# Down projection by seven half products instead of eight, with four weight sums made in DRAM

## The chip, the cores and the metric

One core of a Trainium2 chip runs the whole kernel as one program. It has five engines, each with its own instruction stream: TensorE (PE in the rows; PEld is its loading of weights), VectorE (DVE), ScalarE (ACT), GpSimd (POOL) and SyncE (SP), which issues transfers. Instructions of an engine run in the order written; engines wait for each other by semaphores. Data lies in SBUF (128 partitions), in PSUM (eight banks of 128x512 fp32 that TensorE writes), and in DRAM. The metric is device microseconds of one execution.

## The reference

One layer of a decoder on 1024 tokens of width 1024: a mixer, then a gated MLP. The change touches the last product of the MLP and the addition behind it:

```python
def conv_gated_mlp(x, w_up, conv_w, w_down):
    h = causal_dwconv(x @ w_up, conv_w)
    gt, val = jnp.split(h, 2, axis=-1)
    return (jax.nn.silu(gt) * val) @ w_down
...
x = x + rms_norm(conv_gated_mlp(h, ffn_w_up[l], ffn_conv_w[l], ffn_w_down[l]), norm_ffn_post[l])
```

The inner width is 2816, so the last product is (1024 x 2816) times (2816 x 1024), in fp32. rms_norm divides each row of 1024 by its root mean square and multiplies by a gain.

## The kernel before, in words

An fp32 product is done as two passes of a reduced format: a weight tile w is split into a high part (ScalarE copies it with a scale, `dn_split_hi`, L2306) and a low part (w minus the high part, `dn_split_lo`, L2316, on VectorE or POOL); the activations likewise (`act_split_hi`, L2351, on ScalarE; `act_split_lo`, L2355, on VectorE). A pair of matmuls, high by high and low by low with the scales chosen so that both add to the product, goes into a PSUM bank (`pair`, L2490).

The down projection takes the tokens in two halves of four tiles (m = 0, 1) and the inner width in 22 blocks of 128 (k). A step kk = (m, k) loads 128x1024 weights from DRAM, splits them, splits 128x512 activations, and does 4 tiles x 2 column halves x 2 parts = 16 matmuls. Two PSUM banks belong to a tile, so a half uses all eight. Weights and activations go through rings of four buffers: the high part of step kk waits until TensorE is through with step kk - 4. The activations of the up projection were spilled to DRAM (`act_mid`) and come back by `act_reload`. In the up projection before it, which is already done by seven products a slab, POOL makes the low parts (`split_mult_lo`, L2102), VectorE the sums of weights from SBUF (`weight_sum`, L2225) and the sums in PSUM (`added`, L2232). The order of the up stage, with the first three steps of the down projection in it, is a list written out by hand (`UP_ORDER`: e loads weights, f and g split them, i and j split activations, t, c, v, y, p are the convolution and gate).

After a half, `norm` (ScalarE) squares and sums a row and takes the inverse root, `finish` (VectorE) multiplies by it and by the gain, `add` adds the input of the MLP (x1r, reloaded from DRAM), and SP stores. The last tile is done in two column halves (L2411 on ScalarE, L2442 and L2450 on VectorE), the last but one by POOL (`down_pool`, L2481).

In the mixer, POOL's part for token tile t (0 to 7) begins with `A1b` (`scaled`, L1005, twice), then `A3a` (L1028, L1030, and L1032 behind ScalarE's L1168) and `B1` (L1022, used by VectorE's L1346). SP issues the small transfers of the mixer (L915, L927).

## Time and profile before

| | us |
|---|---|
| three runs: lowest, median, highest | 1059.56, 1063.14, 1063.42 |
| the profiled execution | 1061.33 |
| its span | 1059.6 |
| TensorE busy | 1023.5 (97%) |
| VectorE busy | 814.0 (77%) |
| ScalarE busy | 634.9 (60%) |
| POOL busy | 500.8 (47%) |

A busy time is the time in which an engine had an instruction running; TensorE's instructions overlap, so two matmuls may stand 0.23 us apart and be listed with 0.39 each. A line's idle time before it is put down to what released it last.

### The profile page before, as it was taken

Reading aid. Unit: us, or ns where it says so; the run is one execution under the profiler, and the core shown is the slowest. Engines: PE = TensorE matmul, PEld = TensorE weight load, DVE = VectorE, ACT = ScalarE, POOL = GpSimd, SP = SyncE. Lnnn points to the kernel's source line nnn. Section 1 sums busy time; section 2 is a strip of 40 time slices with the busy share of each in tenths; the row PEclk is TensorE's granted clock in tenths of the full one; section 3 lists DMA queues with packets and bytes.
Section 4 is the critical chain, followed back from the end, with each engine's and each line's share of the span. In section 5 each row is a group of like instructions: output and inputs, shape, how many; then the busy total and the mean of one; then the engine's idle time right before and its main releaser. Section 6 shows DMA issues by size and latency. Waiting matters only on the chain.

```text
span 1059.6 us, 19099 instructions
## 1 busy us (share of the span) xinstructions
PE 1023.5 (97%) x7136; PEld 831.5 (78%) x7136; DVE 814.0 (77%) x1140; ACT 634.9 (60%) x1201; POOL 500.8 (47%) x653
## 2 busy tenths in 40 slices
PE   5999999998999999999999999999999998999997
PEld 4878878986777778777688787888887786888885
DVE  5798895756668886877586598899999999646755
ACT  7544423347777777777865455666666667446443
POOL 2457423726454565551410278788788886000000
PEclk9999999999999999999999999999999999999999
DMA  8245311352122112012263612234433335955962
GB/s 274 71 128 171 115 52 27 75 121 58 41 60 60 36 44 60 19 29 61 90 222 126 199 41 80 80 123 129 130 126 122 121 110 210 371 170 182 331 240 80
DMA packets 159523, 126.78 MB, mean 120 GB/s; under 512 B 63908, under 2 KB 137928, under 8 KB 159432
## 3 DMA queue, kind: packets, MB, share of 16 engines
q1 hardware_dynamic: 157992, 120.32, 37.8%
q10 hardware_dynamic: 1440, 5.24, 1.2%
q8 instruction: 58, 0.95, 0.4%
q14 instruction: 33, 0.27, 0.1%
HBM read 99.79 MB, written 25.71 MB: 118 GB/s over the span
## 4 chain that ended last, share of the span: by engine, by line
PE 57%; DVE 9%; issue 4%; POOL 4%; ACT 3%; DMA 0%; DVEq 0%; ACTq 0%; POOLq 0%
PE psum L2490 14%; PE psum L2278 9%; PE psum L1786 5%; PE psum L1735 5%; PE psum L1719 4%; POOL slab_q L2102 4%; PE psum L1551 4%; PE psum L1901 3%; PE psum L1702 3%; PE psum L2284 2%; DVE arena L2186 2%; DVE arena L2180 1%; DVE arena L2225 1%; DVE psum L2232 1%; PE psum L1632 1%
## 5 line engine op out<-in xcount | busy, mean ns | idle before, releaser
L2102 POOL TENSOR_TENSOR slab_q<-arena,slab_p 128x512 fp32r<-128x512 f32 x127 | 208.2, 1668 | 45.5 <-ACT slab_p L2095 45.4
L2490 PE MATMUL psum<-dn_p,ap_p 128*128 128x512 f32 x352 | 110.3, 393 | 2.7 <-DVE arena L2186 1.4
L2490 PE MATMUL psum<-dn_q,ap_q 128*128 128x512 f32 x352 | 109.8, 391 | 0.0
L2278 PE MATMUL psum<-t_p,slab_p 128*128 128x512 f32 x272 | 106.3, 391 | 1.3 <-ACT arena L2159 0.8
L2278 PE MATMUL psum<-t_q,slab_q 128*128 128x512 f32 x272 | 105.9, 389 | 0.0
L2095 ACT ACTIVATE slab_p<-arena 128x512 fp32r<-128x512 f32 x127 | 78.2, 628 | 38.7 <-PE psum L2278 13.8
L2316 DVE TENSOR_TENSOR dn_q<-arena,dn_p 128x1024 fp32r<-128x1024 f32 x41 | 50.2, 1224 | 56.3 <-ACT dn_p L2306 56.3
L1431 DVE CUSTOM_DVE_ANT_0 psum<-psum,arena 128x640 f32<-128x640 f32 (+7 forms) x96 | 67.8, 717 | 29.8 <-PE psum L1702 29.2
L2306 ACT ACTIVATE dn_p<-arena 128x1024 fp32r<-128x1024 f32 x44 | 46.6, 1059 | 70.0 <-PE psum L2490 65.6
L3066 PE MATMUL psum<-h_p,cm_p 128*128 128x512 f32 (+1 forms) x288 | 86.4, 372 | 0.6 <-DVE arena L2973 0.6
L3066 PE MATMUL psum<-h_q,cm_q 128*128 128x512 f32 (+1 forms) x288 | 85.8, 371 | 0.0
L2278 PE MATMUL psum<-h_p,slab_p 128*128 128x512 f32 x204 | 79.8, 391 | 0.7 <-POOL slab_q L2102 0.6
L2490 PEld LDWEIGHTS psum<-dn_p,ap_p 128*128 128x128 f32 x352 | 65.7, 188 | 18.8 <-issue 2.5
L1219 ACT ACTIVATE arena<-psum,arena 128x640 f32<-128x640 f32 (+7 forms) x96 | 67.1, 701 | 21.5 <-DVE arena L1431 20.7
L2278 PE MATMUL psum<-h_q,slab_q 128*128 128x512 f32 x204 | 79.4, 389 | 0.0
L2481 POOL TENSOR_TENSOR arena<-arena 128x1024 f32<-128x1024 f32 x1 | 2.4, 2356 | 160.6 <-DVE arena L2454 160.6
L2490 PEld LDWEIGHTS psum<-dn_q,ap_q 128*128 128x128 f32 x352 | 66.1, 188 | 14.6
L2951 DVE SCALAR_TENSOR_TENSOR arena<-psum,arena 128x1023 f32<-128x1023 f32 (+29 forms) x60 | 75.9, 1265 | 1.4
L1226 ACT ACTIVATE arena<-psum 128x384 f32<-128x384 f32 x132 | 60.1, 488 | 22.6 <-PE psum L1719 21.3
L2225 DVE TENSOR_TENSOR arena<-arena 128x512 f32<-128x512 f32 x68 | 72.6, 1083 | 0.0
L2591 POOL TENSOR_TENSOR cm_q<-arena,cm_p 128x1024 fp32r<-128x1024 f32 x16 | 39.1, 2443 | 60.8 <-ACT cm_p L2586 60.7
L1735 PE MATMUL psum<-arena 128*64 128x192 f32 x528 | 63.4, 345 | 1.7 <-ACT arena L1226 1.7
(321 smaller groups left out, 2632.3 us busy)
## 6 DMA issues: line engine op xcount, KB each, us to landing
arena<-in_ffn_w_up SPq DMA_DIRECT2D x44, 512.0 KB, 5.2
arena<-in_ffn_w_down SPq DMA_DIRECT2D x44, 512.0 KB, 4.0
arena<-in_w_in SPq DMA_DIRECT2D x20, 512.0 KB, 3.9
act_mid<-arena SPq DMA_DIRECT2D x18, 512.0 KB, 2.6
arena<-act_mid SPq DMA_DIRECT2D x36, 256.0 KB, 5.0
arena<-in_x SPq DMA_DIRECT2D x16, 512.0 KB, 4.8
qkv_mid<-arena ACTq DMA_DIRECT2D x9, 512.0 KB
arena<-qkv_mid SPq DMA_DIRECT2D x8, 576.0 KB, 4.6
```

The source lines that it names most:

```text
L1219: act.activation(probs(u), s_psum(u, n), ACT.Exp, scale=-1.0, bias=nmx[:, u % 2:u % 2 + 1], accum_out=psums[:, NH * kind + h:NH * kind + h ...
L1226: act.activation(pt[x % 2].rearrange("p g c -> p (g c)"), psum[:, bank, 0:GDIM], ACT.Copy).then_inc(done, 1)
L1431: v.tensor_tensor_reduce(out=s_psum(u, n), in0=s_psum(u, n), in1=hidden, scale=-1.0, scalar=-NEG, op0=ALU.add, op1=ALU.min, accum_out=nmx[ ...
L1735: ins = pe.matmul(psum[tok, 7, 0:GDIM // 2], val[:, b, kind, HD * kv:HD * (kv + 1)], pt[x % 2][:, :, tok], start=b == k0, stop=True, skip_ ...
L1786: ins = pe.matmul(wm_ps[WM_SLOT[t]][:, n * 512:(n + 1) * 512], x[:, k], w[:, n * 512:(n + 1) * 512], start=first and k == ks[0] and w is w ...
L2095: act.activation(slab_p[n % RING], part_source(i, j), ACT.Copy, scale=1.0 - SPLIT_W).then_inc(late("up_hi")[0], 1)
L2102: pool.tensor_tensor(slab_q[n % RING], part_source(i, j), slab_p[n % RING], ALU.subtract).then_inc(late("up_lo")[0], 1)
L2225: v.tensor_tensor(out, x, y, op).then_inc(late("s_add")[0], 1)
L2278: ins = pe.matmul(mult_ps(i, j), w[:, k], x[:, k], start=k == 0 and x is x_p[i] and i in (1, 2, 5), stop=True, skip_group_check=True)
L2490: ins = pe.matmul(dn_ps[t % HT][:, n * 512:(n + 1) * 512], x[:, tok], w[:, n * 512:(n + 1) * 512], start=first and x is ap_p[s], stop=True ...
L2951: own.up(v.scalar_tensor_tensor(out=cacc[:, c, s:S], in0=glu[c][:, 0:S - s], scalar=w, in1=cacc[:, c, s:S], op0=ALU.mult, op1=ALU.add))
L3066: ins = pe.matmul(cm_ps[i % 2][:, c0:c1], w[:, k], x[:, k, c0:c1], start=k == 0 and x is h_p, stop=True, skip_group_check=True)
```

## The change

The down projection is written as a 2x2 block product: tokens in two halves, the inner width in two halves of 11 blocks (HK = 11), the columns of the result in two halves of 512. By Strassen's scheme in Winograd's form seven products of half matrices replace eight. They are taken in the order 1, 2, 6, 5, 7, 3, 4, each of 11 steps, so a step n runs from 0 to 76. A step loads 128x512 weights, splits them and 128x512 activations, and does 4 tiles x 2 parts = 8 matmuls of the same shape as before. Weight buffers are a ring of eight half tiles, activation buffers still one of four.

The products need sums of blocks on both sides. The four sums of weights are made in DRAM (`w_sums`, four arrays of 1408x512 fp32, 2.88 MB each) by eight transfers that POOL issues in the mixer, right after `A1b` of tiles 0, 2, 4, 5, 6 and 7: copies, and transfers that add to what lies there. The sums of activations are made in place in SBUF in steps 16 to 27: on VectorE `third` (L2536) and `second` (L2545), on POOL `minus` (L2605) and `fourth` (L2610). The weights' low parts are POOL's in steps 0 to 15 and in every even step from 40, VectorE's else (L2366 on either; L2435 is now `act_split_lo`).

Two sets of four PSUM banks take the products in turn. Between products ScalarE copies a set to SBUF (`copied_out`) or VectorE adds what was copied to it and writes a quarter of the result (`joined`, L2551, L2554, L2558). Squares and row sums come quarter by quarter (L2496 on ScalarE), and POOL multiplies by the gain (`weighted`, L2614). At the end POOL adds two sums of squares (L2631) and two tiles of the input (L2637); VectorE finishes two tiles of the first half (L2582) and all of the second (L2591 from PSUM, L2598). The first six steps stand in the hand-written order of the up stage, where three stood.

```diff
+HK = NF // 2
+DN_MULTS = (1, 2, 6, 5, 7, 3, 4)
+DN_STEPS = [(i, k) for i in DN_MULTS for k in range(HK)]
+DN = len(DN_STEPS)
+W_RING, A_RING = 8, 4
+UP_TAIL = 6
+DN_POOL_LO = [n for n in range(DN) if n < 16 or (n >= 40 and n % 2 == 0)]
+DN_DVE_LO = [n for n in range(DN) if n not in DN_POOL_LO]
...
-    "h3.21 i0 l3.21 e1 a2.21 f0 v0.20 i1 g0 k7.21 v1.20 y20 a5.21 i2 p20 f1 t1.21 g1 j0 j1 x20 f2 a3.21 c1.21 t0.21 g2 v1.21 c0.21 "
-    "v0.21 y21 p21 "
+    "h3.21 i0 l3.21 a2.21 f0 f1 b0 v0.20 i1 g0 g1 k7.21 v1.20 y20 a5.21 e2 e3 i2 p20 b1 t1.21 j0 j1 x20 e4 e5 f2 j2 g2 i3 f3 g3 a3.21 "
+    "j3 c1.21 t0.21 i4 f4 g4 j4 v1.21 i5 f5 g5 j5 c0.21 v0.21 y21 p21 "
...
+        def down_sums(pool, t):
+
+            w11, w12, w21, w22 = [a["ffn_w_down"][0, h * HK * P:(h + 1) * HK * P, c * HALF_D:(c + 1) * HALF_D] for h in range(2) for c in range(2)]
+            one, two, three, four = [w_sums[n] for n in range(4)]
+            if t == 0:
+                pool.dma_start(one, w11).then_inc(sem("wt"), 16)
+                pool.dma_start(three, w12).then_inc(sem("wt"), 16)
+            elif t == 2:
+                pool.wait_ge(sem("wt"), 32)
+                pool.dma_start(one, w12, accum_op=ALU.add).then_inc(sem("wt"), 16)
+                pool.dma_start(three, w22, accum_op=ALU.add).then_inc(sem("wt"), 16)
+            elif t == 4:
+                pool.wait_ge(sem("wt"), 64)
+                pool.dma_start(two, one).then_inc(sem("wt"), 16)
+            elif t == 5:
+                pool.wait_ge(sem("wt"), 80)
+                pool.dma_start(two, w22, accum_op=ALU.add).then_inc(sem("wt"), 16)
...
                 scaled(kg[t % 2], kn, EG, t).then_inc(sem("g_kk2"), 1)
+                down_sums(pool, t)
...
+            if n >= A_RING:
+                act.wait_ge(*late("dn_mm", n - A_RING + 1))
...
+            def third(k):
+                act_landed(v, 0, k)
+                act_landed(v, 1, k)
+                v.tensor_tensor(quarter(0, k), quarter(0, k), quarter(1, k), ALU.subtract).then_inc(late("d_s")[0], 1)
...
+            for n in range(UP_TAIL, DN):
+                for i, at_ in ((2, 26), (7, 59), (3, 70)):
+                    if at_ <= n < at_ + 2:
+                        joined(i, 2 * (n - at_))
+                        joined(i, 2 * (n - at_) + 1)
+                if n in DN_DVE_LO:
+                    dn_split_lo(v, n)
+                act_split_lo(v, n)
+                if 16 <= n < 16 + HK:
+                    third(n - 16)
+                if 17 <= n < 17 + HK:
+                    second(n - 17)
...
+            def minus(k):
+                row_sum_done(pool, "S3", k)
+                act_landed(pool, 1, k + HK)
+                pool.tensor_tensor(quarter(1, k), quarter(1, k + HK), quarter(1, k), ALU.subtract).then_inc(late("d_z")[0], 1)
+
+            def fourth(k):
+                row_sum_done(pool, "S2", k)
+                pool.wait_ge(*late("ap_lo", DN_STEPS.index((2, k)) + 1))
+                pool.tensor_tensor(quarter(0, k + HK), s2[k % len(s2)], quarter(0, k + HK), ALU.subtract).then_inc(late("d_z")[0], 1)
...
+            for n in range(UP_TAIL, 40):
+                if n in DN_POOL_LO:
+                    dn_split_lo(pool, n)
+                if 17 <= n < 17 + HK:
+                    minus(n - 17)
+                    fourth(n - 17)
...
+            pool.wait_ge(*late("f_sq", 3 * HT))
+            pool.tensor_tensor(wrs[:, 2 * HT:3 * HT], wss[:, 0:HT], wss[:, HT:2 * HT], ALU.add).then_inc(late("f_b")[0], 1)
+            for t in range(HT):
+                weighted(c12[t], 2 * HT + t + 1, right_d)
...
+            own_k = 4
+            for n in range(DN - own_k):
+                i, k = DN_STEPS[n]
+                ready(n)
+                for t in range(HT):
+                    if k == 0:
+                        free(i, t)
+                    ins = pair(n, t, k == 0 and i in (1, 2, 5))
+                ins.then_inc(late("dn_mm")[0], 1)
+            for t in range(HT):
+                for n in range(DN - own_k, DN):
+                    if t == 0:
+                        ready(n)
+                    ins = pair(n, t, False)
+                ins.then_inc(late("dn_t")[0], 1)
```

What stands on VectorE in the middle of the down projection before, for some two steps (dn_p and dn_q are the high and low part of the weights, ap_p and ap_q of the activations; arena is any other SBUF; the number behind a name tells the buffers apart):

```order
L2316 TENSOR_TENSOR dn_q_146<-arena,dn_p_142 128x1024
L2355 SCALAR_TENSOR_TENSOR ap_q_154<-ap_p_150,arena 128x512
L2462 TENSOR_TENSOR arena<-arena 128x1024
L2316 TENSOR_TENSOR dn_q_147<-arena,dn_p_143 128x1024
L2355 SCALAR_TENSOR_TENSOR ap_q_155<-ap_p_151,arena 128x512
```

And on VectorE in steps 17 and on now:

```order
L2366 TENSOR_TENSOR dn_q_154<-arena,dn_p_146 128x512
L2435 SCALAR_TENSOR_TENSOR ap_q_162<-ap_p_158,arena 128x512
L2536 TENSOR_TENSOR arena<-arena 128x512
L2545 TENSOR_TENSOR arena<-arena 128x512
L2366 TENSOR_TENSOR dn_q_155<-arena,dn_p_147 128x512
L2435 SCALAR_TENSOR_TENSOR ap_q_163<-ap_p_159,arena 128x512
```

Where a step had one instruction for its weights and one for its activations, and only now and then an addition, a step of half the matmuls now has four.

POOL from the end of the up projection to its last instruction before, where the additions to the last but one tile (L2481) are all that it does after three low parts of weights:

```order
L2102 TENSOR_TENSOR slab_q_171<-arena,slab_p_166 128x512
L2316 TENSOR_TENSOR dn_q_145<-arena,dn_p_141 128x1024
L2316 TENSOR_TENSOR dn_q_146<-arena,dn_p_142 128x1024
L2316 TENSOR_TENSOR dn_q_147<-arena,dn_p_143 128x1024
L2481 TENSOR_TENSOR arena<-arena 128x1024
```

POOL now, around step 15:

```order
L2366 TENSOR_TENSOR dn_q_154<-arena,dn_p_146 128x512
L2366 TENSOR_TENSOR dn_q_155<-arena,dn_p_147 128x512
L2366 TENSOR_TENSOR dn_q_156<-arena,dn_p_148 128x512
L2605 TENSOR_TENSOR arena<-arena 128x512
L2610 TENSOR_TENSOR arena<-arena 128x512
```

And at the end of its program, from step 73 on:

```order
L2614 TENSOR_TENSOR arena<-arena 128x512
L2366 TENSOR_TENSOR dn_q_151<-arena,dn_p_143 128x512
L2366 TENSOR_TENSOR dn_q_153<-arena,dn_p_145 128x512
L2631 TENSOR_TENSOR arena<-arena 128x4
L2614 TENSOR_TENSOR arena<-arena 128x512 x4
L2637 TENSOR_TENSOR arena<-arena 128x1024 x2
```

POOL has instructions through the whole stage now: low parts of weights, eleven pairs of L2605 and L2610 in a row, products with the gain, and at the very end seven instructions in a chain.

POOL at token tile 0 of the mixer before (L1028 and L1030 are `A3a`):

```order
L1002 TENSOR_TENSOR arena<-arena 128x32
L1011 TENSOR_TENSOR arena<-arena 128x48
L1005 TENSOR_TENSOR arena<-arena 128x384 x2
L1028 TENSOR_TENSOR arena<-arena 128x384
L1030 TENSOR_TENSOR arena<-arena 128x384
```

And now, where the same lines are L1050, L1074 and L1076:

```order
L1047 TENSOR_TENSOR arena<-arena 128x32
L1056 TENSOR_TENSOR arena<-arena 128x48
L1050 TENSOR_TENSOR arena<-arena 128x384 x2
L1019 DMA w_sums<-in_ffn_w_down 1408x512
L1020 DMA w_sums<-in_ffn_w_down 1408x512
L1074 TENSOR_TENSOR arena<-arena 128x384
L1076 TENSOR_TENSOR arena<-arena 128x384
```

Two issues of 1408 rows of 512 stand in front of what used to follow at once.

## Rows read from the trace of the kernel before

**Rows 1.** Page, part 1: span; busy time, share and instructions of each engine.

```profile
span 1059.6 us, 19099 instructions
PE 1023.5 (97%) x7136; PEld 831.5 (78%) x7136; DVE 814.0 (77%) x1140; ACT 634.9 (60%) x1201; POOL 500.8 (47%) x653
```

**Rows 2.** Chain of waits, in order: start us, us, what; the down projection.

```profile
898.65 139.32 PE psum L2490 x608
1041.12 12.24 PE psum L2490 x52
```

**Rows 3.** Windows, down: PE, PEld, DVE, ACT, POOL busy (count); clock, DMA, GB/s.

```profile
888.00:898.00 10.00, 8.31 (x33) 5.59 (x31) 8.80 (x8) 4.01 (x5) 4.20 (x2) 1.00 0.82 278
898.00:1038.00 140.00, 139.35 (x609) 114.47 (x610) 82.55 (x89) 69.08 (x96) 0.00 (x0) 1.00 0.70 253
1038.00:1053.40 15.40, 14.95 (x64) 11.56 (x62) 8.79 (x9) 7.14 (x17) 0.58 (x1) 1.00 0.17 69
1053.40:1059.60 6.20, 0.00 (x0) 0.00 (x0) 2.29 (x3) 1.16 (x4) 1.78 (x1) 0.70 0.44 169
```

**Rows 4.** Page, part 5: the down projection's matmuls, one of two forms.

```profile
L2490 PE MATMUL psum<-dn_p,ap_p 128*128 128x512 f32 x352 | 110.3, 393 | 2.7 <-DVE arena L2186 1.4
```

**Rows 5.** Timeline, the end of the down stage; idle time and releaser in brackets.

```profile
1041.09 0.30 PEld L2490 LDWEIGHTS psum<-dn_p,ap_p 128*128 128x128 f32 x2 [0.78 <-DVE dn_q L2316]
1052.82 2.36 POOL L2481 TENSOR_TENSOR arena<-arena 128x1024 f32<-128x1024 f32 x1 [160.62 <-DVE arena L2454]
1052.95 0.39 PE L2490 MATMUL psum<-dn_q,ap_q 128*128 128x512 f32 x1
1054.70 1.68 DVE L2450 SCALAR_TENSOR_TENSOR arena<-arena 128x512 f32<-128x512 f32 x2
```

**Rows 6.** Single lines: ns least/median/greatest, first and last start, form.

```profile
L2225 DVE TENSOR_TENSOR arena<-arena x68: 674/937/1820, 658.6 to 879.8; 128x512 f32<-128x512 f32 x68
L2232 DVE TENSOR_TENSOR psum<-psum,arena x51: 681/686/700, 675.7 to 889.9; 128x512 f32<-128x512 f32 x51
L2102 POOL TENSOR_TENSOR slab_q<-arena,slab_p x127: 1282/1527/3380, 617.7 to 881.6; 128x512 fp32r<-128x512 f32 x127
L2355 DVE SCALAR_TENSOR_TENSOR ap_q<-ap_p,arena x44: 682/684/2896, 886.4 to 1040.3; 128x512 fp32r<-128x512 f32 x44
L2095 ACT ACTIVATE slab_p<-arena x127: 613/631/637, 613.3 to 880.6; 128x512 fp32r<-128x512 f32 x127
```

**Rows 7.** Timeline of POOL and VectorE (DVE), 872 to 883 us: start, us, instruction.

```profile
872.89 10.00 POOL L2102 TENSOR_TENSOR slab_q<-arena,slab_p 128x512 fp32r<-128x512 f32 x6 [2.47 <-ACT slab_p L2095]
873.47 2.97 DVE L2225 TENSOR_TENSOR arena<-arena 128x512 f32<-128x512 f32 x2
```

**Rows 8.** Timeline, mixer, around the places of POOL's new transfers.

```profile
234.66 1.00 POOL L1030 TENSOR_TENSOR arena<-arena 128x384 f32<-128x384 f32 x1
236.43 0.51 ACT L1168 ACTIVATE arena<-arena 128x384 f32<-128x384 f32 x1
289.21 0.83 POOL L1022 TENSOR_TENSOR arena<-arena 128x384 f32<-128x384 f32 x1 [3.72 <-PE psum L1612]
293.48 0.74 DVE L1346 TENSOR_TENSOR arena<-arena,psum 64x192 f32<-64x192 f32 x2 [0.60 <-PE psum L1623]
387.78 1.61 POOL L1005 TENSOR_TENSOR arena<-arena 128x384 f32<-128x384 f32 x2 [1.70 <-DVE arena L1300]
422.29 1.62 POOL L1005 TENSOR_TENSOR arena<-arena 128x384 f32<-128x384 f32 x2 [3.97 <-DVE arena L1300]
```

**Rows 9.** Issue of transfers on SP: ns least/median/greatest.

```profile
L915 SPq DMA_DIRECT2D arena<-tri_mid x8: 308/331/1556, 241.9 to 466.0; - x8
L927 SPq DMA_DIRECT2D arena<-inv_mid x16: 580/612/627, 258.5 to 482.8; - x16
```

**Rows 10.** Windows, early mixer (columns as in Rows 3).

```profile
250.00:255.00 5.00, 3.71 (x23) 2.14 (x21) 3.49 (x12) 4.34 (x15) 4.09 (x14) 0.88 0.00 0
254.00:255.00 1.00, 1.00 (x8) 0.68 (x4) 0.00 (x0) 0.95 (x5) 0.73 (x4) 0.50 0.00 0
```

More of the change, by code:

```diff
@@ new lines, in down_loads @@
+            for t in (0, 1):
+                sp.wait_ge(sem("fin_v"), t + 1)
+                sp.dma_start(out[0, t * P:(t + 1) * P, :], y_dn[:, t]).then_inc(sem("stored"), 16)
+            for t in (2, 3):
+                sp.wait_ge(*late("fin_p", t - 1))
+                sp.dma_start(out[0, t * P:(t + 1) * P, :], y_dn[:, t]).then_inc(sem("stored"), 16)
+            for t in range(HT, NT - 1):
+                sp.wait_ge(sem("fin_v"), t - 1)
+                sp.dma_start(out[0, t * P:(t + 1) * P, :], y_dn[:, t]).then_inc(sem("stored"), 16)
@@ new lines, in copied_out, with squares @@
+            def copied_out(i, t):
+                product_done(act, i)
+                if i == 1 and t == 0:
+                    act.wait_ge(*late("up_mm", 2 * CLASSIC + PRODUCTS))
+                act.activation({1: c11, 6: c12, 5: c22}[i][t], acc_of(i)[t], ACT.Copy).then_inc(late("e_cp")[0], 1)
+            def squares(n, x, before):
+                if before:
+                    act.wait_ge(*late("f_sq", before))
+                act.activation(junk2[:, left_d], x, ACT.Square, accum_out=wss[:, n:n + 1]).then_inc(late("f_sq")[0], 1)
```

464 lines of the change are left out of this document (250 added, 214 removed), and 2 rows, old and new, of the table UP_ORDER.

## The prediction

> **What bounds the kernel now.** I read the page first, then the chain of waits, then the windows of the down projection, then single lines by duration, and last the timelines of VectorE and POOL side by side. The page has TensorE busy for 97% of the span, so only two things move the time: fewer or cheaper matmuls, and gaps between them [rows 1]. The chain shows the down projection as one run of TensorE: 608 matmuls in 139.32 us, 0.229 us each, and after one short stop 52 more [rows 2]. All its 704 matmuls (two forms of 352) stand between 888.0 and 1053.4 us [rows 3, 4]. 704 x 0.229 is 161.3 us, so 4.1 of these 165.4 us are gaps, 1.7 of them in the first 10 us (8.31 of 10 busy). POOL has nothing to do from 898 to 1052 us, VectorE is 59% busy, ScalarE 49% [rows 3]. The last VectorE instruction ends at 1056.4, 3.0 us after the last matmul, and the store of that half ends the span at 1059.6 [rows 5].
>
> **What is removed.** Seven products of eleven steps n, each of four token tiles and two matmuls: 616 matmuls against 704, of the same 128x512 form. 88 x 0.229 = -20.2 us. A step is 8 x 0.229 = 1.83 us of TensorE. Product 1 needs only the four banks of the second last slab, where the old order soon came to the banks of the last one; I keep 1 us of the 4.1 us of gaps for the new head (bounds 0 and 4.1): -3.1 us.
>
> **What is added on VectorE and POOL, and what it collides with.** This is the term that decides. First what they charge alone: a two-input VectorE instruction of 128x512 takes 0.67 to 0.68 us (least of L2225, median of L2355), and starts about 0.60 after the one in front, as they overlap a little; a POOL one 1.28 us (least of L2102), 1.25 from start to start [rows 6]. But L2225 reaches 1.82 us and L2102 has a median of 1.53. The timelines say why: POOL needs 10.0 us for six instructions that alone take 7.7, and inside that stretch two L2225 in a row take 2.97 us instead of 1.35 [rows 7]. Each of the two waited for a POOL instruction to end, and POOL waited in turn. L2232, which reads one operand from PSUM and one from SBUF, stays between 0.681 and 0.700 in all 51 cases although POOL is as busy [rows 6]. So I add the times of instructions with two SBUF inputs on VectorE and of POOL's, one after the other, wherever both have work; before, POOL had none in this stretch.
>
> Steps 17 to 27. VectorE has four such instructions a step (weight low part, activation low part, L2536, L2545), POOL two (L2605, L2610), and POOL's two wait for VectorE's two of the same step, so neither can be put off far. That is 4 x 0.60 + 2 x 1.25 = 4.9 us a step where TensorE wants 1.83. Eleven steps: 53.9 us against 20.2. The ring of four activation buffers lets VectorE be three steps ahead, 5.5 us. +28.2 us. Bounds: without any lead +33.7; if VectorE never waited for POOL, 11 x 2.4 = 26.4, and 2.4 for the four additions from PSUM that fall in steps 26 and 27, less 20.2 and 5.5: +3. I take the upper half, since the rows show the pair taking turns.
>
> The Trainium skill speaks against the change here: "SBUF — State Buffer", section "Who interferes with whom", says that a VectorE instruction with two SBUF inputs and a POOL instruction that reads SBUF hold a shared port by turns, each for its whole length, and that with one SBUF input VectorE does not meet POOL at all. The 2.97 us and the steady 0.69 us agree. By a reading in which both only slow each other a little, this term would be the +3 above.
>
> Steps 59 to 74. Activation low part 0.60, every other step a weight low part on VectorE (0.60) or POOL (1.25), every other step one L2614 on POOL (1.25): 2.15 us a step on average, 0.32 over TensorE's 1.83, sixteen times, less what lead is left: +4 us (0 to 5). Steps 28 to 58 need 1.2 to 1.6 us and hide behind TensorE; so do ScalarE's two splits a step (0.63 each at most) and its 12 copies and 12 squares.
>
> Last four steps. TensorE takes them tile by tile and wants all four activation buffers at once, which are freed only by step 72; the old kernel stops there for 0.8 us on the weight side [rows 5]. With the port shared, I take 2.5 us more (0 to 3.8).
>
> **The end.** POOL's L2631 needs the squares of the last quarter, which ScalarE issues in steps 73 to 76, some 8 us before TensorE ends. Behind it stand on POOL four L2614 (1.25 each) and two additions of 128x1024 (2.36 by L2481 [rows 5]), 9.7 us; on VectorE two L2582 and three L2598 of 128x1024 (1.2 each, double the 0.60) and two halves, 7.2 us. All read two SBUF operands. 17 us of turns from -7.4 end at +9.6, with the multiplications from PSUM between them at about +11.5, against +3.0 before: +8.5 us (bounds: +4, where only ScalarE's and VectorE's own chains count, and +12).
>
> **The sums of weights.** Eight transfers of 2.88 MB are issued by POOL during the mixer. Does POOL wait for them? A copy reads and writes 5.8 MB, an accumulation reads twice and writes, 8.7 MB; at the 253 GB/s of the down stage [rows 3] that is 23 and 34 us. The tightest step, from tile 5 to tile 6, is 34.5 us (387.78 to 422.29 [rows 8]), for one accumulation. So no wait or a very short one. What the issue costs POOL is not in the trace, since no transfer of before is issued there. The nearest rows are SP's: 0.33 us for one of 48 x 16 runs, 0.61 for one of 64 x 6 [rows 9]; the far bound is the time in which POOL would walk over the same elements, 1408x512 over 128 partitions at 2.36 us per 1024, 13 us. I take 2 us for each of the six with 1408 rows, nearer SP's, and 1 us for the two flat copies. Behind them stand on POOL: at tile 0 L1028 and L1030, whose result ScalarE's L1168 uses 0.8 us after they end, so 2 x 2 us come out as 3; at tile 2 L1022, which has 3.7 us of idle ahead of it and 3.4 us behind it until VectorE's L1346 wants it, so nothing comes out [rows 8]; at the other four about 1 us together. +4 us (0 to 62).
>
> The Trainium skill's "DMA: Bandwidth & Descriptors", section "Anatomy of one DMA — SWDGE (gpsimd) path", calls the generation of descriptors small and variable and gives 2.0 us and bytes over 436e3 for a transfer; by that alone this term would be near 0. No row here shows it.
>
> **TensorE's clock.** In the mixer the granted clock fell to 0.50, the 1.2 GHz level, for some 3.5 us around 255 us, in a stretch in which TensorE was busy for 3.71 of 5 us [rows 10]. In steps 17 to 27 it will be busy for 1.83 of 4.9. At half speed a step is 3.7 us, still under 4.9, so nothing is lost there; the first microseconds behind it may run at half: +1 us (0 to 5).
>
> **Sum.** -20.2 - 3.1 + 28.2 + 4 + 2.5 + 8.5 + 4 + 1 = +24.9 us on the profiled execution of 1061.33 us (its span of 1059.6 and 1.7 around it; the median of the runs shown is 1.8 above it): 1086 us.
>
> **Rivals.**
> The two engines do not hold each other up, because VectorE's instructions go first or POOL's fall into its gaps. Then the terms are -20.2 - 3.1 + 3 + 0 + 0 + 4 + 4 + 0 = -12.3: 1049 us. For it: the rows show waits where POOL had come first, not who wins when both stand ready, and L2610's result is wanted only from step 55. Against it: L2610 and L2605 stand on POOL in front of the weight parts of step 40 and are ready to run at once, so they do run there. 17%. Half blocked, it would lie within 5 us of before: 8%.
>
> Issuing from POOL is dear. At 13 us for each of the six, tile 0 shows 25, tile 2 19 (26 less 7), tiles 5 and 7 about 11 each: 66 us instead of 4, 1148 us; it decides from some 3.5 us each, where the 7 us of room at tile 2 are used up; at 6 us each it is 25 us and 1107. For it: POOL has no row that says otherwise. Against it: SP's rows do not grow with the number of runs. 15%.
>
> The forecast itself: 60%. That the sums come too late is no case: the last is issued at tile 7 of the mixer, and the first load that needs one comes in step 22 of the down projection, hundreds of microseconds later.
>
> **Chances and range.** Below 0.5% (5 us) a measurement of this kernel can hardly tell a change from none. Faster 18% (the first rival), within 0.5% 8%, slower 74%. The forecast's own range is 1068 to 1105 (its terms at their inner bounds). The range runs down to the first rival and into the second: 1050 to 1118.
>
> **What would show it.** In the profile after: 616 matmuls still 0.229 us apart where TensorE runs freely; L2536 and L2545 on VectorE well above 0.68 us on average, L2605 and L2610 above 1.28; TensorE near 40% busy for about 48 us in the second fifth of the down stage, waiting for VectorE's activation or weight low parts; the down stage some 177 us from first to last matmul; some 14 us from the last matmul to the end. L2366 and L2435 at 0.68 us throughout and no gap in TensorE would prove the first rival; idle ScalarE or TensorE at 234 and 286 us, behind POOL's transfers, the second. I am wrong if POOL's instructions run without holding VectorE up, or if the mixer grows by more than 10 us.

## The result, and the profile after

The changed kernel takes 1146.70 us (median of 4 runs, 1146.43 to 1147.66) against 1062.81 for the kernel before in the same comparison: a ratio of 1.080 with a 95% interval of 1.078 to 1.082. Slower was forecast, but 1086 us, and 1146.7 is outside the range of 1050 to 1118.

The page of the changed kernel, part 1, answers to [rows 1]: span, then busy time, share and instructions of each engine.

```profile
span 1145.9 us, 19413 instructions
PE 1032.9 (90%) x7048; PEld 832.1 (73%) x7048; DVE 881.6 (77%) x1202; ACT 661.7 (58%) x1289; POOL 612.0 (53%) x729
```

88 matmuls are gone, and yet TensorE idles for 113 us instead of 36. Where, four marks tell: the first matmul of the output projection, the first and the last of the down projection, and the end of the span.

| us from the span's start | before | after | difference |
|---|---|---|---|
| output projection starts | 524.9 | 589.7 | +64.8 |
| down projection starts | 888.0 | 953.1 | +65.1 |
| down projection, first to last matmul | 165.4 | 178.0 | +12.6 |
| from there to the end | 6.2 | 14.8 | +8.6 |

So 65 of the 86 us come from the mixer, where the change only adds eight transfers. The mixer as one window of each kernel (columns as in [rows 3]); first before, then after:

```profile
225.00:524.90 299.90, 291.59 (x3732) 226.70 (x3726) 217.15 (x552) 221.93 (x577) 149.23 (x334) 0.99 0.22 50
```

```profile
225.00:589.70 364.70, 308.99 (x3740) 240.40 (x3734) 221.84 (x552) 222.66 (x577) 157.20 (x342) 0.90 0.47 105
```

VectorE, ScalarE and POOL do the same work as before to within 8 us; TensorE's busy time grows by 17 us at a lower granted clock (0.90 instead of 0.99). What doubled is the DMA side. The waits of the changed kernel from 225 to 640 us (who waited for whom: us in total, times, the longest), and below them the first one as it was before:

```profile
POOL arena L1090 <- DMA arena<-tri_mid: 62.1, 5, 17.4
ACT arena L1265 <- DVE arena L1477: 53.7, 28, 20.3
...
PE psum L1597 <- DMA arena<-invt_mid: 33.2, 3, 19.0
```

```profile
POOL arena L1044 <- DMA arena<-tri_mid: 27.8, 5, 7.6
```

The mixer sends small triangles to DRAM and back within its chain (`tri_blocks` and `inverse_back`, on SP's queue). While a bulk transfer runs, they come back late. The timeline of the changed kernel around POOL's second pair of bulk transfers; POOL issues two accumulations, then SP stores the inverse and loads it again only 21 us later:

```profile
298.88 1.53 POOL L1023 DMA_DIRECT2D w_sums<-in_ffn_w_down  x1
299.80 2.14 POOL L1024 DMA_DIRECT2D w_sums<-in_ffn_w_down  x1
...
305.94 0.30 SPq L942 DMA_DIRECT2D inv_mid<-arena  x1
306.28 0.54 SPq L942 DMA_DIRECT2D invt_mid<-arena  x1
327.35 1.25 SPq L948 DMA_DIRECT2D arena<-inv_mid  x2
```

How long the eight pairs of stores of the inverse took to land, after and before:

```profile
DMA to landing us min/median/max: 1.9/2.2/21.0
...
DMA to landing us min/median/max: 1.9/2.1/2.2
```

The store of tri_mid landed in 2.3 / 5.4 / 15.2 us against 2.3 / 2.3 / 3.7. The DMA queues of the changed kernel show why; q0 is POOL's, q1 SP's (packets, MB, and the time of the packets as a share of the 16 engines' time, above 100% where packets overlap), from 306 to 310 us, from 315 to 320 and from 320 to 325:

```profile
q0 software_dynamic: 366, 0.75, 109.7%
q1 hardware_dynamic: 17, 0.00, 0.7%
...
q0 software_dynamic: 504, 1.00, 108.3%
q1 hardware_dynamic: 504, 0.03, 15.8%
...
q0 software_dynamic: 496, 1.02, 109.1%
q1 hardware_dynamic: 496, 0.03, 15.5%
```

In the last two stretches the two queues move packet for packet. A small store of 48 KB in runs of 16 numbers is 768 packets of 64 bytes; each waits for one packet of 2 KB. 1536 of them, for the two stores, at 100 a microsecond are 15 us. In the kernel before, the same queue moved 1155 packets of such a pair in the one microsecond from 257 to 258. The Trainium skill says this in "DMA: Bandwidth & Descriptors", section "Queues, rings and completion order": each DMA engine goes round its queues packet by packet. The trace agrees, with 504 to 504.

Turns do not explain all of it. From 306 to 310 us SP's queue moved only 17 packets, although both stores had been issued by 306.8: some 4 of the 21 us pass before the packets begin. And beside the first two copies SP's queue moved 216 packets to POOL's 439 from 240 to 246 us, and only then, from 246 to 252, as many as POOL's (473 to 475).

The rest of the profile came out near the forecast. The down projection of the changed kernel in windows (columns as in [rows 3], whose stage they answer to):

```profile
953.00:985.00 32.00, 28.39 (x118) 22.85 (x117) 28.24 (x23) 21.93 (x38) 22.18 (x14) 0.95 0.92 326
985.00:1035.00 50.00, 32.81 (x108) 23.24 (x107) 50.00 (x50) 16.12 (x28) 35.08 (x22) 0.83 0.43 138
1035.00:1060.00 25.00, 24.17 (x106) 19.55 (x105) 18.93 (x29) 16.60 (x30) 3.52 (x3) 1.00 0.52 157
1060.00:1090.00 30.00, 30.00 (x133) 24.57 (x132) 19.09 (x25) 22.75 (x45) 12.15 (x10) 1.00 0.49 168
1090.00:1131.00 41.00, 38.86 (x161) 29.01 (x159) 39.08 (x37) 25.65 (x52) 32.65 (x21) 1.00 0.44 160
1131.00:1145.90 14.90, 0.08 (x1) 0.00 (x0) 9.50 (x9) 5.55 (x17) 5.28 (x3) 0.64 0.62 247
```

From 985 to 1035 us VectorE is busy for all 50 us and TensorE has matmuls in flight for 32.8. Its instructions there, of the changed kernel (ns least/median/greatest, first and last start), answer to [rows 6]: L2435 is the activations' low part, L2536 `third`, L2605 `minus`, L2610 `fourth`, L2551 the addition that reads PSUM.

```profile
L2435 DVE SCALAR_TENSOR_TENSOR ap_q<-ap_p,arena x77: 674/693/1852, 951.5 to 1123.1; 128x512 fp32r<-128x512 f32 x77
L2536 DVE TENSOR_TENSOR arena<-arena x11: 679/1761/1781, 984.4 to 1028.7; 128x512 f32<-128x512 f32 x11
L2605 POOL TENSOR_TENSOR arena<-arena x11: 1673/1724/1740, 985.2 to 1031.3; 128x512 f32<-128x512 f32 x11
L2610 POOL TENSOR_TENSOR arena<-arena x11: 1279/1652/1674, 988.7 to 1034.3; 128x512 f32<-128x512 f32 x11
L2551 DVE TENSOR_TENSOR arena<-psum,arena x4: 675/676/679, 1025.1 to 1030.5; 128x512 f32<-128x512 f32 x4
```

`third` takes 1.76 us instead of 0.68 beside `minus`, while L2551, which reads PSUM, keeps 0.68 in the same stretch.

The end answers to [rows 5]. POOL's timeline of the changed kernel (`weighted`, L2614, and the last additions, L2637), then ScalarE's (scaling of finished tiles, L2521, and squares, L2496), then VectorE's first finishing of a tile of the second half (L2598):

```profile
1124.69 6.98 POOL L2614 TENSOR_TENSOR arena<-arena 128x512 f32<-128x512 f32 x4
1131.64 4.63 POOL L2637 TENSOR_TENSOR arena<-arena 128x1024 f32<-128x1024 f32 x2
```

```profile
1131.71 1.15 ACT L2521 ACTIVATE arena<-arena 128x1024 f32<-128x1024 f32 x1 [1.00 <-POOL arena L2614]
1132.76 0.58 ACT L2496 ACTIVATE arena<-psum 128x512 f32<-128x512 f32 x1
```

```profile
1134.34 3.02 DVE L2598 SCALAR_TENSOR_TENSOR arena<-arena 128x1024 f32<-128x1024 f32 x1
```

ScalarE's first square of the last four tiles waits behind a scaling, and that for POOL, until 1.7 us after the last matmul has ended (1131.1). L2598, beside POOL's L2637, takes 3.02 us; the next two of its kind, with POOL at rest, take 1.28 each.

### The profile page after: what moved, and what is told of

The parts are those of the page before. It is cut to its first block and busy times, and to the rows that moved or that the text cites. A ratio compares the mean times of both kernels' runs of the same rounds, so it can differ in the third digit from the quotient of the medians.

```text
span 1145.9 us, 19413 instructions
## 1 busy us (share of the span) xinstructions
PE 1032.9 (90%) x7048; PEld 832.1 (73%) x7048; DVE 881.6 (77%) x1202; ACT 661.7 (58%) x1289; POOL 612.0 (53%) x729
## 5 line engine op out<-in xcount | busy, mean ns | idle before, releaser
L2648 PE MATMUL psum<-dn_p,ap_p 128*128 128x512 f32 x308 | 127.1, 413 | 23.8 <-DVE ap_q L2435 22.1
L2648 PE MATMUL psum<-dn_q,ap_q 128*128 128x512 f32 x308 | 125.1, 406 | 0.0
L2435 DVE SCALAR_TENSOR_TENSOR ap_q<-ap_p,arena 128x512 fp32r<-128x512 f32 x77 | 86.0, 1131 | 17.9 <-ACT ap_p L2431 17.7
L2648 PEld LDWEIGHTS psum<-dn_p,ap_p 128*128 128x128 f32 x308 | 60.4, 196 | 45.8 <-issue 25.8
L2431 ACT ACTIVATE ap_p<-arena 128x512 fp32r<-128x512 f32 x77 | 48.6, 631 | 61.9 <-PE psum L2648 51.3
L2366 POOL TENSOR_TENSOR dn_q<-arena,dn_p 128x512 fp32r<-128x512 f32 x35 | 52.0, 1497 | 57.5 <-ACT dn_p L2362 57.5
L1597 PE MATMUL psum<-arena 64*64 64x64 f32 x1152 | 48.4, 239 | 33.4 <-DMA arena<-invt_mid 33.2
L1597 PEld LDWEIGHTS psum<-arena 64*64 64x64 f32 x1152 | 42.4, 151 | 42.5 <-issue 40.6
L1765 PE MATMUL psum<-arena 128*128 128x128 f32 x396 | 64.7, 292 | 7.9 <-DVE arena L1490 7.2
```

What stands on the lines that cost most here:

```text
L1597: ins = pe.matmul(out[rows, h * CH:(h + 1) * CH], lhs[rows, h], rhs[rows, h], start=start, stop=True, skip_group_check=True)
L1765: ins = pe.transpose(psum[:, bank, g * P:(g + 1) * P], probs(u + g)[:, (b - k0) * P:(b - k0 + 1) * P], ident)
L2435: v.scalar_tensor_tensor(out=ap_q[n % A_RING], in0=ap_p[n % A_RING], scalar=1.0 - 1.0 / SPLIT_W, in1=act_part(n), op0=ALU.mult, op1=ALU.su ...
L2648: ins = pe.matmul(acc_of(i)[t], x[:, tok], w, start=first and x is ap_p[n % A_RING], stop=True, skip_group_check=True)
```

## The experiments

Theory A: the bytes of the bulk transfers on the shared DMA engines hold up the mixer's small transfers. Against it B (POOL's issuing or its waits) and C (accumulation as such). Theory D: VectorE and POOL take turns in steps 17 to 27. Against it E (VectorE's own load). All runs in one table: the marks of the profiled run, and the median time of 2 to 10 runs (before: 1063 to 1064 in each comparison). e1, e2 and e16 put plain blocks of weights in place of the sums, e3 and e4 leave parts of the sums out, so their output is not the reference's; the matmuls are the same in number and form.

| run | output proj. starts | down proj. starts | its length | to the end | time |
|---|---|---|---|---|---|
| after | 589.7 | 953.1 | 178.0 | 14.8 | 1146.7 |
| e1_no_sums | 525.6 | 889.0 | 180.3 | 14.9 | 1087.0 |
| e2_thin | 531.5 | 895.0 | 180.5 | 14.9 | 1091.8 |
| e3_plain | 569.5 | 933.1 | 179.1 | 14.9 | 1127.1 |
| e4_no_pool_sums | 586.9 | 950.5 | 156.9 | 14.9 | 1127.2 |
| e5_short_rows | 619.2 | 983.0 | 179.8 | 14.9 | 1180.1 |
| e6_moved | 526.0 | 939.1 | 178.9 | 14.9 | 1135.8 |
| e7_dve | 590.2 | 954.5 | 160.9 | 14.9 | 1132.1 |
| e8_both | 527.4 | 939.6 | 164.9 | 14.9 | 1120.1 |
| e9_pairs | 525.2 | 918.1 | 179.8 | 14.9 | 1114.2 |
| e10_tail | 589.2 | 952.7 | 185.6 | 8.6 | 1147.3 |
| e11_all | 524.2 | 915.0 | 168.3 | 10.2 | 1093.6 |
| e12_early | 560.4 | 923.8 | 180.7 | 14.8 | 1118.8 |
| e13_early_all | 560.7 | 924.8 | 163.8 | 11.4 | 1100.4 |
| e14_early_spread | 560.5 | 923.6 | 162.9 | 11.4 | 1098.9 |
| e15_cover | 533.1 | 916.8 | 165.1 | 11.4 | 1091.6 |
| e16_free_sums | 527.2 | 890.7 | 163.5 | 11.4 | 1067.2 |

**e1_no_sums.**

```diff
-                down_sums(pool, t)
...
-                return w_sums[WSUM_OF[i], k * P:(k + 1) * P, :]
+                return a["ffn_w_down"][0, k * P:(k + 1) * P, right_d if i in (5, 6) else left_d]
```

> Leaves out the eight transfers that make the sums of weights, and SyncE's wait for them; the four products that used the sums load plain blocks of the down weights instead, so the output is not the reference's. Everything else of the changed kernel stays. If the 65 us that the mixer became longer come from the sums of weights in any way, the output projection starts near 525 us again instead of 590 and the time is about 1146.7 - 65 = 1082 us (1078 to 1088). If something else of the change lengthened the mixer (another buffer, another place in memory), it stays near 1147 us.

1087.0 us, and the output projection starts at 525.6 again. The 65 us are the sums' (64.1 by this mark; 59.7 in the median time, and 2.3 of the difference because the down stage is longer in this run's profile). The rest of the change costs 23 us, where the forecast had 21 (24.9 without its 4 for the sums).

**e2_thin.**

```diff
-            one, two, three, four = [w_sums[n] for n in range(4)]
+            one, two, three, four = [w_sums[n][:, 0:16] for n in range(4)]
+            w11, w12, w21, w22 = [w[:, 0:16] for w in (w11, w12, w21, w22)]
...
```

> The same eight transfers of 1408 rows with the same waits and semaphores, but 16 columns of each row instead of 512: a 32nd of the bytes, the same number of rows to describe and of issues by GpSimd; the products load plain blocks of weights (the sums are left out of the computation). Theory A, that the bytes of the bulk transfers on the shared DMA engines hold up the mixer's small transfers: about 1085 us (1080 to 1095), stores of tri_mid land in 2.3 to 4 us again. Rival B, that GpSimd's issuing, the making of the descriptors or GpSimd's waits for the sums hold it up: 1140 to 1147 us. In between would mean that the number of rows counts as well as their bytes.

1091.8 us: with the same issues, waits and rows the mixer pays 6.6 us instead of 64.8. The transfers land sooner here, too, but in the changed kernel none of POOL's listed waits from 225 to 640 us is for one of them. So B falls. The DMA part of its page (KB each, median us to landing):

```profile
tri_mid<-arena SPq DMA_DIRECT2D x16, 96.0 KB, 2.3
...
w_sums<-in_ffn_w_down POOLq DMA_DIRECT2D x6, 88.0 KB, 4.2
```

**e3_plain.**

```diff
-                pool.dma_start(one, w12, accum_op=ALU.add).then_inc(sem("wt"), 16)
+                pool.dma_start(one, w12).then_inc(sem("wt"), 16)
...
```

> All eight transfers with all their bytes and waits, but as plain copies, none accumulating (sums left incomplete). In the trace an accumulating transfer lands after about 21 us and a plain one after 10.8 us when each runs alone. Theory A (bulk time on the DMA engines): the bulk's time falls from some 150 us to some 100 us, and the 65 us to about 40 to 45, so 1120 to 1127 us. Rival C, that only accumulation holds the small transfers up: 1082 to 1090 us. Rival B (issue and waits of GpSimd): 1146 us, or a little less because the waits end earlier.

1127.1 us; the mixer pays 44.6 us. The cost grows with the time for which the bulk occupies the engines: the eight landing times add up to 121.5 us here and to 152.2 in the changed kernel. C falls as the whole cause. Its DMA rows:

```profile
w_sums<-in_ffn_w_down POOLq DMA_DIRECT2D x6, 2816.0 KB, 14.5
...
tri_mid<-arena SPq DMA_DIRECT2D x16, 96.0 KB, 4.0
```

**e4_no_pool_sums.**

```diff
...
-                if 17 <= n < 17 + HK:
-                    minus(n - 17)
-                    fourth(n - 17)
```

> Leaves out the two sums of activations that GpSimd makes in each of steps 17 to 27 of the down projection (minus and fourth); the products 5 and 3 use unsummed rows. VectorE's own four instructions in a step stay. Theory D (VectorE and GpSimd take turns at their operands): VectorE's instructions there fall from 1.1 us to 0.68 us, a step from 4.9 us to 4 x 0.68 = 2.7 us, so 11 x 2.2 = 24 us less: the down projection takes 154 us from first to last matmul instead of 178, the time is about 1123 us (1119 to 1127). Rival E (VectorE is slow there by its own load alone): its instructions stay at 1.1 us and more, and the time at 1142 to 1147 us.

The stage takes 156.9 us instead of 178.0. Without POOL beside them, `third` and `second` (L2536, L2543 of this run) take 0.68 us each:

```profile
L2536 DVE TENSOR_TENSOR arena<-arena x11: 679/682/685, 982.6 to 1007.3; 128x512 f32<-128x512 f32 x11
L2543 DVE TENSOR_TENSOR arena<-arena x11: 679/682/683, 985.0 to 1010.9; 128x512 f32<-128x512 f32 x11
```

D holds with 21 us of the 24 expected, and E falls as the main cause. The edit also takes away VectorE's waits for `fourth`; in the changed kernel VectorE was busy for all 50 us from 985 to 1035, so it lost nothing to such waits.

**e5_short_rows.**

```diff
+            def short(out, x, **how):
+                for c in range(0, HALF_D, P):
+                    pool.dma_start(out[:, c:c + P], x[:, c:c + P], **how).then_inc(sem("wt"), 16)
...
```

> The changed kernel with the same sums and the same bytes, but each transfer cut into four of 128 columns, so that a packet of the bulk is 512 bytes instead of 2 KB or more; 32 issues instead of 8, at the same eight places. In the trace of the changed kernel the two queues move packet for packet while a bulk transfer runs (496 and 496 packets in 320 to 325 us), so a small transfer waits one bulk packet for each of its own. Theory A1 (packets in turn): with a bulk packet of about a quarter of the time, the stores of tri_mid and inv_mid that fall beside the bulk land in 4 to 9 us instead of 15 to 21, and the stalls shrink from 65 us to about 20. The 24 more issues at 0.6 to 2.1 us cost GpSimd up to 30 us, of which the mixer may show 5 to 20: together 1110 to 1130 us. Theory A2 (the small transfers share bandwidth, or stand behind the whole bulk): the stores land in 15 to 21 us as before and the time is 1150 us or more.

Neither forecast holds: the time, 1180.1 us, misses, and the landing times do not decide. The greatest of the inverse's store falls from 21.0 to 7.6 us, of tri_mid's from 15.2 to 11.4, which looks like packets taken in turn. But the store that took 7.6 us, issued at 345.5, moved its first packets behind 349 us, when the bulk was at its end (from 350 to 351 SP's queue moved 1068 packets, POOL's 137). And beside tri_mid's stores the edit hardly shortened the bulk's packets: from 248 to 252 us 331 packets carried 1.25 MB, 3.8 KB each, against 4.1 in the changed kernel (316 and 1.29 MB). So the turns stay untested by this run. What made it slower is new: POOL stands still between its issues, for nothing that the profile names. From this run's waits (225 to 640 us):

```profile
POOL w_sums L1021 <- issue: 43.5, 5, 12.3
```

32 issues of 1408 short rows in groups of four and eight were too many in flight, as it seems; that was not tried further.

**e6_moved** puts 32 pieces of 352 rows beside the up projection; **e7_dve** gives the 22 sums to VectorE; **e8_both** does both.

```diff
...
+            if n >= 8 and (n - 8) % 3 == 0 and (n - 8) // 3 < 32:
+                down_sums(pool, (n - 8) // 3)
```

```diff
...
+                if n == 26:
+                    fourth(0)
+                if 28 <= n < 28 + HK:
+                    minus(n - 28)
+                if 40 <= n < 39 + HK:
+                    fourth(n - 39)
```

> The changed kernel with the same eight sums, but each transfer cut into four of 352 rows, and the 32 pieces issued by GpSimd one by one during the up projection (after every third of its split products, from the ninth on), none in the mixer. Theory A: the output projection starts near 525 us again, the up projection takes its pieces without loss because its loads are asked for ahead, and the time is that without the sums, 1087 us, up to 1095 with some of GpSimd's issue time showing. Rival: the bulk costs what it costs wherever it stands (the memory, or GpSimd's issuing, is the bound), and the up projection becomes 40 to 65 us longer: 1127 to 1150 us.

> The changed kernel with GpSimd's 22 sums of activations in steps 17 to 27 given to VectorE and spread: the first fourth in step 26, the minus ones in steps 28 to 38, the other fourth ones in steps 40 to 49. Sums of weights as in the changed kernel. Theory D (turns): VectorE's instructions cost 0.68 us again in steps 17 to 27, the 22 more at 0.68 us lie mostly in slack, and the down projection takes 158 us (154 to 163) instead of 178: about 1127 us. Rival E (VectorE's own load is what costs): 15 us more work for VectorE make it 1146 to 1160 us.

> The last two together: the sums of weights in 32 pieces during the up projection, and the 22 sums of activations on VectorE. If the two causes are separate and add up, 1087 - 20 = 1067 us (1060 to 1075), which is the time of the kernel before within 1 per cent; if they hide each other, 1080 us or more.

e7: the stage takes 160.9 us, 17 less, although VectorE has 22 instructions more. e6: the mixer is free (526.0), but the up projection is 50 us longer. Its waits from 520 to 940 us name POOL itself, waiting for the piece before in front of splits that TensorE needs, and the up projection's own loads:

```profile
POOL w_sums L1024 <- DMA w_sums<-in_ffn_w_down: 48.7, 19, 5.8
...
ACT slab_p L2130 <- DMA arena<-in_ffn_w_up: 12.1, 7, 3.8
```

e8 carries the same 50 us, hence 1120 and not 1067. In e1, without any pieces, the waits for the loads of the up projection come to 6.7 us.

**e9_pairs** waits two pieces back, **e10_tail** rearranges the end, **e11_all** has all three.

```diff
...
+            wt = sem(("wt", "wt1")[p % 2])
+            if n:
+                pool.wait_ge(wt, 16 * (p // 2))
```

```diff
...
+                if n >= 75:
+                    for t in (2 * n - 150, 2 * n - 149):
+                        v.tensor_tensor(c12[t], c12[t], gpost_ffn[:, right_d], ALU.mult).then_inc(late("e_cp")[0], 1)
...
-            for t in range(2):
+            for t in range(HT):
                 half_one(t)
```

> As the run with the 32 pieces during the up projection, but without its wait: there GpSimd stood 48.7 us in 19 waits for the piece before, in front of the splits that TensorE needs. Now six pieces are issued at the end of the output projection's work on GpSimd (which is idle there for 47 us), the others after every fourth split product, and each waits only for the piece two before it. Theory F, that the 48 us of the earlier run were that wait: 1088 us (1086 to 1095). Rival G, that the up projection's own loads come late beside the pieces whatever GpSimd does (they ended 18.8 us of waits in that run): 1100 to 1110 us. Rival H, that bulk bytes cost the same in any stage: 1130 us or more.

> The changed kernel, sums of weights in the mixer as they were, with the end rearranged: ScalarE squares the right upper quarter one step earlier and no longer scales two finished tiles before the last squares; VectorE weights the right upper quarter in steps 75 and 76 and finishes all eight tiles, GpSimd has nothing after its last split. In the trace of the changed kernel the last tile's chain stood behind GpSimd's weighting (4 x 1.75 us, until 1131.67), and a 1024-wide VectorE instruction took 2.23 us beside GpSimd instead of 1.28. Expected: from the last matmul's start to the end 9 to 10 us instead of 15.2, so 1141 to 1142 us. If the end is bound by the chain of square, logarithm and exponent alone, 1145 us or more.

> All three together: the sums of weights in 32 pieces beside the output and up projections without the wait, the 22 sums of activations on VectorE, and the rearranged end. If the causes are separate, 1088 - 16 - 5 = 1067 us by the first run's level, against 1062.7 for the kernel before; 1060 to 1072. If the loads of the up projection come late, 1075 to 1090.

e9: 21 us came back, 29 stay in the up projection; 1114.2 us lies between the ranges of G and H. Its waits from 520 to 925 us show the loads late, as in G, and some of POOL's waits left:

```profile
ACT slab_p L2131 <- DMA arena<-in_ffn_w_up: 13.7, 4, 6.6
POOL w_sums L1025 <- DMA w_sums<-in_ffn_w_down: 13.0, 2, 10.4
...
ACT up_p L2104 <- DMA arena<-in_ffn_w_up: 11.4, 5, 3.2
```

e10 gained 6.2 us behind the last matmul, the most that was expected, and lost 7.6 ahead of it. VectorE's weighting in steps 75 and 76 stands in front of the last activation split, which starts 177.0 us behind the stage's first matmul here (1129.69) and 170.0 in the changed kernel (1123.1). From VectorE's timeline of this run; L2435 is the activation split, L2581 the weighting:

```profile
1126.72 1.77 DVE L2435 SCALAR_TENSOR_TENSOR ap_q<-ap_p,arena 128x512 fp32r<-128x512 f32 x1
1128.41 0.15 DVE L2578 TENSOR_TENSOR arena<-arena 128x4 f32<-128x4 f32 x1
1128.49 1.28 DVE L2581 TENSOR_TENSOR arena<-arena 128x512 f32<-128x512 f32 x2
1129.69 0.68 DVE L2435 SCALAR_TENSOR_TENSOR ap_q<-ap_p,arena 128x512 fp32r<-128x512 f32 x1
```

The weighting itself accounts for 1.3 of these 7 us. VectorE was 2.7 us behind already at step 70, which the edit does not touch; the rest is not accounted for.

e11 takes 1093.6 us, outside both of its ranges: the stretch from the output projection to the down projection is 27 us longer than in e1, and the down stage takes 168.3 us where e8, with the old end, has 164.9.

**e12_early** puts the pieces into the first stage, **e13_early_all** adds VectorE's sums and an end that weights after the last split, **e14_early_spread** thins VectorE's steps out.

```diff
...
                     split_lo(pool, n)
+                    if pieces and n >= 9:
+                        down_sums(pool, pieces.pop(0))
```

```diff
...
+                for k in range(HK):
+                    if n == 16 + 6 * k // 5:
+                        third(k)
+                for k in range(HK):
+                    if n == 17 + 6 * k // 5:
+                        second(k)
```

> The changed kernel with the same 32 pieces of the sums, issued by GpSimd in the first stage (input projections, between 65 and 205 us), each waiting for the piece two before it, none in the mixer or later. In the run without the sums the DMA engines were 0.20, 0.19, 0.15 and 0.06 busy in the four stretches from 120 to 200 us and no engine of the chain waited for a load there. Theory A (the bulk costs only where transfers on the path meet it): the output projection starts at 525 to 530 us, the time is 1087 us (1085 to 1095). Theory H (it costs 27 us or more wherever it stands): 1114 us or more.

> The same early pieces, with the 22 sums of activations on VectorE, and an end in which VectorE finishes all eight tiles but weights the right upper quarter only after its last split (in the earlier run of the end it did so in steps 75 and 76, which delayed the last matmul by 7.6 us and gave the gain back). By separate terms: 1087 - 16 - 3 = 1068 us (1062 to 1074), within 1 per cent of the kernel before. If the early pieces cost the first stage, 1080 us or more.

> As the run before it, with VectorE's four instructions in each of steps 16 to 27 thinned out: third and second in five of every six steps from 16 and 17 to 29, the minus ones in 30 to 40, the other fourth ones in 42 to 51. VectorE's load there falls from 4 x 0.68 = 2.7 us a step to 3.7 x 0.68 = 2.5, against 1.83 of TensorE: 11 x 0.2 = 2 us less than the run before it, 1066 us (1060 to 1073). If the order of these sums does not bind, the same as the run before it.

e12's windows show both sides. From 80 to 120 us the bulk runs beside a TensorE that misses nothing; from 160 to 180, where POOL waits for pieces ahead of the sums that the keys and queries need, TensorE stands:

```profile
80.00:100.00 20.00, 20.00 (x88) 16.22 (x87) 17.40 (x15) 10.34 (x11) 14.96 (x22) 1.00 0.90 305
100.00:120.00 20.00, 20.00 (x88) 16.22 (x87) 16.54 (x14) 9.03 (x9) 16.01 (x68) 1.00 0.85 258
...
160.00:180.00 20.00, 8.44 (x34) 7.03 (x35) 6.96 (x9) 3.66 (x8) 9.08 (x12) 0.66 0.94 206
```

The 32 pieces ran on until 235 us and cost 34.8 us in all, as theory H had it. e13 and e14 inherit that; the end that weights late keeps 3.4 us (11.4 against 14.8) at no loss in the stage (163.8 against e8's 164.9), and thinning out gives 0.9 us of stage, within what two profiles differ by.

**e15_cover** spreads the pieces over three stages, **e16_free_sums** leaves them out and keeps e14's rest.

```diff
...
+                    for p in range(14, 18) if n == 19 else range(n - 5, n - 4) if 5 <= n < 19 else ():
+                        down_sums(pool, p)
...
+            for p in range(18, 26):
+                down_sums(pool, p)
```

> As the last run (22 sums on VectorE, thinned out; end finished by VectorE), with the 32 pieces placed anew: fourteen in the input projections after a split each (46 to 120 us), four more before GpSimd's idle 20 us there, eight in GpSimd's idle 48 us of the output projection, six in the up projection, one after every sixteenth split product. Theory A: the mixer starts at its old time, the output projection near 525 us, the first matmul of the down projection near 890 us, then 162.7 us to its last and 11.6 to the end as in the last run: 1064 us span, 1066 us time (1061 to 1073). Theory H (27 us or more wherever the bulk stands): 1090 us or more.

> Leaves out the transfers that make the sums of weights (the four products that used them load plain blocks of the down weights), and keeps the 22 sums of activations on VectorE, thinned out, and the end finished by VectorE. A bound for every placement of the sums: the first matmul of the down projection near 889 us as in the first run, then 162.7 us to the last and 11.6 to the end: a span of 1063.6 us and a time of 1065 us (1061 to 1069), level with the kernel before at 1063. If the sums' loads also hold up the down projection, up to 4 us less, and then a free placement would be faster than the kernel before.

e15, 1091.6 us, is the best version with sums, and the sums still cost 26 us in it (916.8 against 890.7): 6 in or ahead of the mixer, 20 behind it. Its waits from 525 to 930 us name the same two:

```profile
ACT up_p L2104 <- DMA arena<-in_ffn_w_up: 19.5, 5, 8.1
POOL w_sums L1025 <- DMA w_sums<-in_ffn_w_down: 18.6, 4, 7.1
```

Its time lies where H had it. No placement came below 24 us, so a cost of about that size in any stage, whatever it meets there, is not refuted; for A speaks only that the late loads and POOL's waits show in the profile.

e16 takes 1067.2 us against 1063.1, a ratio of 1.0036 (1.0023 to 1.0049). So even sums that cost nothing would leave a kernel of this form no faster than the one before: its stage and end take 174.9 us against 171.6.

## Why the prediction was wrong, and where it was right

**The step that failed is the sums of weights**, "+4 us (0 to 62)"; it measured 65 by the mark and 60 in the time (e1), which is nearly the whole miss of the forecast. The step priced what POOL pays: its issuing and its own waits. That part was right. POOL's issues took 0.57 to 2.14 us each, where 1 and 2 were assumed, no wait of POOL for a sum is among its listed waits in the mixer, and e2, which keeps issues and waits, costs 4.8 us more than e1. What the step left out is everything else that uses the DMA engines. It took no account of them. The stage had room by its averages, 50 GB/s and a DMA share of 0.22. But the mixer's chain goes through small stores and loads on SP that took 2.3 us each, and beside a bulk accumulation one of 768 packets waited for some 768 of the others', so that it landed after 21 us. The bandwidth left over did not help it. From e1 to e3 to the changed kernel the size grows with the bulk's time (0.7, 44.6, 64.8 us), which with e2 shows that the traffic is the cause; that it works packet by packet rests on the queue rows alone, and no run tested it by a time. The bound of 62 was for another mechanism, so it was no cover for this one.

**The rival with the right number was wrong.** "Issuing from POOL is dear" gave 1148 us at 13 us an issue. The rows say 0.57 to 2.14, and e2 excludes it; that its number is nearest is luck.

**TensorE's work and the turns: the mechanism right, the total partly by luck.** The stage was forecast at some 177 us and took 178.0. Take 0.229 us for each matmul of a window and call the rest lost. Some 5 us are lost ahead of 985 us, where the forecast kept 1 for the head: TensorE waits there for VectorE's and POOL's low parts, once for 3.6 us. From 985 to 1035 some 25 are lost, against 28 for the turns and 1 for the clock, and from 1090 on some 4, against 4 + 2.5. So errors of some 4 us cancel. TensorE was busy for 66% of the middle stretch, where the sign named near 40%. The term of +28.2 for steps 17 to 27 rests on VectorE and POOL taking turns; e4 takes POOL out and gives 21.1 us back, e7 moves the work to VectorE and gives 17.1. By the term's own arithmetic VectorE alone at 0.68 us would still be some 4 us too slow there, so 24 was the share to come back; the mechanism holds, its size is off by 3 us. In the middle of the stretch a step takes 4.57 us (`third` starts at 995.42, 999.99 and 1004.57), against 4.9 forecast. The first rival (they do not hold each other up) is excluded by `third` at 1.76 us.

**The end: the size right, the mechanism in part.** 14.8 us against 6.2 + 8.5 forecast. The turns are there: POOL's four weightings take 6.98 us instead of 4 x 1.25, and L2598 3.02 instead of 1.28. But the forecast had only VectorE and POOL taking turns; ScalarE's scaling, which waits for POOL ahead of the last squares, was not in it. e10 takes both away and ends 8.6 us after the last matmul; what each of them costs was not separated.

**The clock: small, as forecast, in the down projection,** where the stretch of steps 17 to 27 had a mean granted clock of 0.83, between its two levels of 1.2 and 2.4 GHz, and VectorE, busy for all 50 us, was the bound there. In the mixer the mean fell from 0.99 to 0.90 behind the new stalls. How much of the 65 us that is was not separated.

**What stays open:** of the 24 to 29 us that well placed pieces still cost (e9, e11, e15), how much is the up projection's late loads and how much POOL's remaining waits, or whether so much is lost wherever the bulk stands; what holds the first packets of a small store back for some 4 us beside the bulk; and whether the mixer would bear the bulk if its own stores were of fewer, longer runs. None of these was tried alone.

## What to carry to other kernels

Before bulk traffic goes into a stage with idle DMA engines, look for small round trips through DRAM on that stage's chain: price them by their packets and the bulk's time for a packet, not by the bandwidth left. A wait for a long transfer belongs where its engine has nothing else to do, or the work behind it pays. And sum the rest first: here 20 us of matmuls saved were outweighed by what VectorE and POOL had to add and by the end, so that, by e16, no placement of the sums alone would have won.

## What was unexpected of the hardware

- An accumulating transfer of 2.88 MB from DRAM to DRAM landed after 20.8 us, a flat copy of the same size after 10.8, and two accumulations in flight after 20.0 and 33.3.
- GpSimd's issue of 1408 rows took 0.9 to 2.1 us, and a 32nd of the bytes did not make it shorter (1.53 and 2.14 us in e2, as in the changed kernel).
- With 32 issues of 1408 short rows, GpSimd stood for 43.5 us between issues (e5).
